# A streaming encoder layer on one core: weights through six 4 KB buffers in place of three of 8 KB

## What is computed

```python
proj = rmsnorm(x, g_mix) @ w_in           # columns q | k | v | g (4 heads x 128) | B | C | h (512 each)
o = rms_scale(retention(rotary(q), rotary(k), v)) * silu(g)     # chunks of 64 frames, a state per head
c = B * short_conv(C * h)                                       # 3 taps
x = x + concat([o, c]) @ w_out
# retrieval, for each frame and each of 8 heads:
q = (rmsnorm(x, g_ffn) @ wq)                     # 1024 x 2048
s1, s2 = q1 @ keys1.T, q2 @ keys2.T              # 128 keys each
eidx, gate = 16 best of the 256 sums of the 16 best of s1 and of s2, softmax
act = gelu(x . u_tab[eidx])                      # 1024 wide rows
x = x + sum(gate * act * v_tab[eidx])
y = rmsnorm(x, g_final)
```

## Time and profile before

| | |
|---|---|
| median of 3 runs | 3038.26 us (3035.58 to 3039.6) |
| the profiled execution | 3035.47 us, of which the span of instructions 3033.6 us |
| granted TensorE clock, mean | 0.846 |
| busy share: PE, PE's weight loads, DVE, ACT, POOL | 76%, 62%, 68%, 67%, 40% |
| moved by DMA | 1226.64 MB, mean 404 GB/s |
| gathers (POOL line 661) | 1056 of 1 MB |
| loads into `stream` | 86 of 1 MB: 26 of w_ret (line 572), 24 of w_conv (line 574), 36 of wq (line 577) |

### The profile page before, as it was taken

One profiled execution on the slowest core, in us unless ns is written; L12 is line 12 of the kernel. 1 busy time (PEld: TensorE's weight loads), 2 busy tenths in 40 slices (PEclk: granted clock), 3 DMA queues, 4 the chain that ended last, 5 costly groups with the idle time before them and its releaser, 6 DMA issues.

```text
span 3033.6 us, 36636 instructions
## 1 busy us (share of the span) xinstructions
PE 2303.3 (76%) x12800; PEld 1880.0 (62%) x12800; DVE 2067.1 (68%) x5112; ACT 2044.8 (67%) x3704; POOL 1228.0 (40%) x1060
## 2 busy tenths in 40 slices
PE   9976887787668887877777877888777766667666
PEld 7765776665557766656566665665556555555555
DVE  2466887566688775666888744566588899955454
ACT  1277666668677566776677666667767777676666
POOL 0133333334333333444443344433344445456653
PEclk9987989998889889987887998989888886666666
DMA  7599999999999999999999999999999999999998
GB/s 301 190 416 397 413 408 414 419 420 413 420 421 409 420 417 415 420 404 420 420 416 406 404 422 419 419 419 396 405 420 420 418 418 409 415 418 419 422 420 333
DMA packets 180568, 1226.64 MB, mean 404 GB/s; under 512 B 20736, under 2 KB 21952, under 8 KB 40736
## 3 DMA queue, kind: packets, MB, share of 16 engines
q0 software_dynamic: 152064, 1107.36, 88.6%
q1 hardware_dynamic: 28032, 116.88, 9.6%
q10 hardware_dynamic: 288, 0.07, 0.0%
HBM read 1219.37 MB, written 4.86 MB: 404 GB/s over the span
## 4 chain that ended last, share of the span: by engine, by line
DMA 35%; DVE 24%; PE 22%; ACT 13%; issue 5%; POOL 1%; DVEq 0%; POOLq 0%; ACTq 0%
DMA ring<-in_uv,idx 35%; DVE ring L1459 12%; PE expert_sum L1116 8%; ACT ring L873 5%; PE mm L914 4%; PE x_ps L976 3%; ACT weights L869 2%; PE mm L1038 2%; PE mm L923 2%; ACT L860 1%; DVE pairs_left L1306 1%; ACT dots L860 1%; DVE pairs_left L1394 1%; DVE top_i L1315 1%; DVE pick_f L1400 1%
## 5 line engine op out<-in xcount | busy, mean ns | idle before, releaser
L661 POOL DMA_INDIRECT ring<-in_uv,idx x1056 | 1227.7, 1163 | 1781.8 <-PE expert_sum L1116 1574.7
L1116 PE MATMUL expert_sum<-ident_sb,ring 128*128 128x128 f32 x8448 | 1367.1, 317 | 581.3 <-ACT ring L873 579.8
L1459 DVE CUSTOM_DVE_ANT_0 ring<-ring,xn 128x1024 f32<-128x1024 f32 x1056 | 1286.7, 1223 | 737.8 <-DMA ring<-in_uv,idx 730.2
L1116 PEld LDWEIGHTS expert_sum<-ident_sb,ring 128*128 128x128 f32 x8448 | 1150.5, 165 | 838.6 <-ACT ring L873 767.9
L873 ACT ACTIVATE ring<-ring,weights 128x1024 f32<-128x1024 f32 x1056 | 1213.2, 1149 | 34.3
L860 ACT ACTIVATE dots<-dots 128x1 f32<-128x1 f32 x1056 | 211.5, 200 | 771.6 <-DVE dots L1459 768.2
L869 ACT ACTIVATE weights<-dots,gate 128x1 f32<-128x1 f32 x1056 | 311.1, 295 | 38.2
L914 PE MATMUL mm<-stream,xn_in 128*128 128x256 f32 (+1 forms) x912 | 258.4, 421 | 71.9 <-ACT qkvg L708 56.3
L1038 PE MATMUL mm<-turn,stream 128*128 128x256 f32 (+2 forms) x1024 | 278.4, 401 | 2.8 <-DVE xn_in L1155 2.8
L914 PEld LDWEIGHTS mm<-stream,xn_in 128*128 128x128 f32 (+1 forms) x912 | 166.9, 199 | 113.7 <-ACT qkvg L708 66.0
L923 PE MATMUL mm<-xn_in,stream 128*128 128x256 f32 (+1 forms) x640 | 183.7, 426 | 34.8 <-ACT conv_tmp L699 22.6
(11 more groups left out here) (233 smaller groups left out, 1517.4 us busy)
## 6 DMA issues: line engine op xcount, KB each, us to landing
stream<-in_wq SPq DMA_DIRECT2D x36, 1024.0 KB, 12.0
stream<-in_w_ret SPq DMA_DIRECT2D x26, 1024.0 KB, 9.4
stream<-in_w_conv SPq DMA_DIRECT2D x24, 1024.0 KB, 11.9
ring<-in_uv,idx POOLq DMA_INDIRECT x1056, 12.3
ring<-in_w_ret SPq DMA_DIRECT2D x7, 1024.0 KB, 12.4
x<-in_x SPq DMA_DIRECT2D x8, 512.0 KB, 8.7
w_out_sb<-in_w_out SPq DMA_DIRECT2D x1, 4096.0 KB, 28.9
out_y<-xn SPq DMA_DIRECT2D x8, 512.0 KB, 11.9
```

What stands on the lines that cost most here:

```text
L661: pool.indirect_dma_start(ring[:, g % RING, :], None, uv, bass.IndirectOffsetOnAxis(ap=rows, axis=0)).then_inc(landed[g % RING], 16)
L1116: ins = pe.matmul(expert_sum[:, c * P:(c + 1) * P], ring[:, g % RING, D + c * P:D + (c + 1) * P], ident_sb[:, :], is_transpose=True, start ...
L1459: dve.tensor_tensor_reduce(u, u, xn[:, t % 3, :], 1.0, 0.0, ALU.mult, ALU.add, dots[:, g % RING:g % RING + 1]).then_inc(dotted, 1)
```

## The change

BUFFERS goes from 3 to 6 and a buffer from 8 KB to 4 KB of a partition. Every item is split: a retention unit into its chunks 0 to 3 and 4 to 7, a convolution pair into its two units, a pass into its halves s = 0 and s = 1. STREAM has 172 items in the order of first use; a second half of a pass is sorted by the slot in which that half begins, both halves of a retention unit by the unit's slot. A half is loaded when the item six before it has been used. The convolution units and the halves of a pass are released one by one, by their own count; the two halves of a retention unit by the same count, at the end of the unit's last use. PE waits for each half where its first chunk stands, also in group 0's units that come through `ring` (there on the same semaphore twice). In the source tensors a half is 4 KB of a partition in one piece.

```diff
--- before.py
+++ after.py
@@ -29,7 +29,7 @@
 QUADS = P // DEC
 TOTAL = TILES * STEPS + STEPS // QUADS
 RING = 7
-BUFFERS = 3
+BUFFERS = 6
 UNIT = 256
 RET_UNITS = 4 * RET // UNIT
 CONV_UNITS = 3 * CH
@@ -251,11 +251,13 @@
 
 
 
+
 STREAM = sorted(
-    [(USES[j][use_at(j, "ret", u, GROUPS[j][0])][3], 0, "ret", j, u) for j in range(1, 4) for u in range(RET_UNITS)]
-    + [(USES[j][use_at(j, "ChB"[2 * i % 3], 2 * i)][3], 0, "conv", j, i) for j in range(4) for i in range(CONV_UNITS // 2)]
-    + [(USES[0][use_at(0, "ret", RING, t)][3], 0, "ret", 0, t) for t in GROUPS[0]]
-    + [(p[3], 1, "wq", n, p[1]) for n, p in enumerate(PASSES)])
+    [(USES[j][use_at(j, "ret", u, GROUPS[j][0])][3], 0, "ret", j, u, s)
+     for j in range(1, 4) for u in range(RET_UNITS) for s in range(2)]
+    + [(USES[j][use_at(j, "ChB"[v % 3], v)][3], 0, "conv", j, v, 0) for j in range(4) for v in range(CONV_UNITS)]
+    + [(USES[0][use_at(0, "ret", RING, t)][3], 0, "ret", 0, t, s) for t in GROUPS[0] for s in range(2)]
+    + [(p[3] + KC * s // p[4], 1, "wq", n, p[1], s) for n, p in enumerate(PASSES) for s in range(2)])
 ITEM = {x[2:]: i for i, x in enumerate(STREAM)}
 
 
@@ -295,7 +297,7 @@
         ring = sb("ring", [P, RING, 2 * D])
         w_out_sb = sb("w_out_sb", [P, KC, D])
         keys_sb = sb("keys_sb", [P, BLK, NK])
-        stream = sb("stream", [P, BUFFERS, 2 * D])
+        stream = sb("stream", [P, BUFFERS, D])
         xn_in = sb("xn_in", [P, KC * wide])
         qkvg = sb("qkvg", [P, 2, 4 * RET])
         conv_out = sb("conv_out", [P, CH, wide])
@@ -550,17 +552,17 @@
 
             def used(i):
 
-                kind, j, n = STREAM[i][2:]
+                kind, j, n, s = STREAM[i][2:]
                 if kind == "wq":
-                    return pass_end(j) - 1, queried, 2 * (j + 1)
+                    return PASSES[j][3] + (KC * (s + 1) - 1) // PASSES[j][4], queried, 2 * j + s + 1
                 if kind == "ret" and j == 0:
                     q = use_at(0, "ret", RING, n)
                     return USES[0][q][3] + 2, projected, q + 1
-                q = use_at(j, "ret", n, GROUPS[j][-1]) if kind == "ret" else use_at(j, "ChB"[(2 * n + 1) % 3], 2 * n + 1)
+                q = use_at(j, "ret", n, GROUPS[j][-1]) if kind == "ret" else use_at(j, "ChB"[n % 3], n)
                 return USES[j][q][3] + 2, projected, USES_BEFORE[j] + q + 1
 
             def load_stream():
-                for i, (_, _, kind, j, n) in enumerate(STREAM):
+                for i, (_, _, kind, j, n, s) in enumerate(STREAM):
                     if i < BUFFERS:
                         yield FIRST
                     else:
@@ -569,13 +571,12 @@
                         sp.wait_ge(semaphore, count)
                     dst = stream[:, i % BUFFERS, :]
                     if kind == "ret":
-                        sp.dma_start(dst, w_ret[n if j else RING]).then_inc(stream_in[i % BUFFERS], 16)
+                        source = w_ret[n if j else RING][:, s * D:(s + 1) * D]
                     elif kind == "conv":
-                        sp.dma_start(dst.rearrange("p (u n) -> p u n", u=2),
-                                     w_conv[2 * n:2 * n + 2].rearrange("u p n -> p u n")).then_inc(stream_in[i % BUFFERS], 16)
+                        source = w_conv[n]
                     else:
-                        sp.dma_start(dst.rearrange("p (b k n) -> p b k n", b=2, k=KC),
-                                     wq[2 * n:2 * n + 2].rearrange("b p k n -> p b k n")).then_inc(stream_in[i % BUFFERS], 16)
+                        source = wq[2 * n + s].rearrange("p k n -> p (k n)")
+                    sp.dma_start(dst, source).then_inc(stream_in[i % BUFFERS], 16)
 
             def load_consts():
                 yield FIRST + 1
@@ -878,13 +879,13 @@
 
         @block.tensor
         def _(pe):
-            def item_in(kind, j, n, t=None):
+            def item_in(kind, j, n, s=0, t=None):
                 if kind == "ret" and j == 0 and n < RING:
                     pe.wait_ge(ret_in[n], 16)
-                    return ring[:, n, :]
+                    return ring[:, n, s * D:(s + 1) * D]
                 if kind == "ret" and j == 0:
                     n = t
-                i = ITEM[kind, j, n]
+                i = ITEM[kind, j, n, s]
                 pe.wait_ge(stream_in[i % BUFFERS], 16 * (i // BUFFERS + 1))
                 return stream[:, i % BUFFERS, :]
 
@@ -905,22 +906,23 @@
                     bank = bank_of(j, q)
                     if kind == "ret":
                         if t == GROUPS[j][0] or j == 0:
-                            weight = item_in("ret", j, unit, t).rearrange("p (k n) -> p k n", k=KC)
+                            weight = [None, None]
                         n, at = rows_of(t), column(t)
                         for k in range(KC):
                             yield slot if slot in range(4) else slot + k // 3
                             if k in (0, KC // 2):
+                                if weight[k // 4] is None:
+                                    weight[k // 4] = item_in("ret", j, unit, k // 4, t).rearrange("p (k n) -> p k n", k=4)
                                 pe.wait_ge(xnT_copied, 2 * x_turn(t) + 1 + k // (KC // 2))
-                            ins = pe.matmul(bank[0:n, 0:UNIT], xnj[:, k, at:at + n], weight[:, k, :],
+                            ins = pe.matmul(bank[0:n, 0:UNIT], xnj[:, k, at:at + n], weight[k // 4][:, k % 4, :],
                                             start=(k == 0), stop=(k == KC - 1))
                     else:
                         if unit == 0:
                             pe.wait_ge(xnT_copied, 2 * x_turn(ORDERS[j][-1]) + 2)
-                        if unit % 2 == 0:
-                            item = item_in("conv", j, unit // 2).rearrange("p (u k n) -> p u k n", u=2, k=KC)
+                        item = item_in("conv", j, unit).rearrange("p (k n) -> p k n", k=KC)
                         for k in range(KC):
                             yield slot + k // 3
-                            ins = pe.matmul(bank[:, 0:w], item[:, unit % 2, k, :], xnj[:, k, :],
+                            ins = pe.matmul(bank[:, 0:w], item[:, k, :], xnj[:, k, :],
                                             start=(k == 0), stop=(k == KC - 1))
                     ins.then_inc(projected, 1)
 
@@ -1031,11 +1033,12 @@
                         by_act, by_dve = taken_all(j)
                         pe.wait_ge(act_took, by_act)
                         pe.wait_ge(dve_took, by_dve)
-                    weight = item_in("wq", m, h).rearrange("p (b k n) -> p b k n", b=2, k=KC)
                     for s in range(2):
+                        yield slot + KC * s // pace
+                        weight = item_in("wq", m, h, s).rearrange("p (k n) -> p k n", k=KC)
                         for k in range(KC):
                             yield slot + (KC * s + k) // pace
-                            ins = pe.matmul(query_bank(m, s), weight[:, s, k, :], xnT_of_pass(m)[:, k, :],
+                            ins = pe.matmul(query_bank(m, s), weight[:, k, :], xnT_of_pass(m)[:, k, :],
                                             start=(k == 0), stop=(k == KC - 1))
                         ins.then_inc(queried, 1)
 
```

## The result

| | before | after |
|---|---|---|
| median | 3036.85 us (22 runs) | 3041.76 us (22 runs) |
| ratio | | 1.0017, 95% interval 1.0011 to 1.0023 |
| the profiled execution, its span | 3035.47, 3033.6 us | 3042.09, 3040.0 us |

The median rose by 4.9 us, inside the 0.2% that I had called no change, with an interval (+3.3 to +7.0 us) that excludes none at all. The forecast had +2.1.

What follows compares the result with a forecast made beforehand. The DMA engines were taken as the bound after about 120 us. Pieces +2.9, completions +0.7, PE's waits 0 and the stall -1.5 sum to +2.1 on a median of 3038.3: 3040.4 us, range 3034.5 to 3046.5.

Steps and rivals of the forecast that it cites:

- The number: Whole kernel: median of three runs 3038.3 us plus 2.1, so 3040.4 us expected; 0.2%, 6 us, counts as no change.
- The bound: Middle of the kernel: the 16 DMA engines are full, share 1.01 at 414 to 416 GB/s; before about 120 us PE bounds.
- PE's added waits: First 120 us, where PE is the bound: 24 added waits cost 0, at most +0.7 us.
- the first gather: Sign at the end of PE's first part: still starts at 119.3 us; over 1 us later would mean the waits cost.
- Smaller pieces, +2.9: The 26 w_ret loads go from 8 KB to 4 KB packets, 1.8 engine-us more each: +2.9 us (2.7 to 3.2).
- Completions, +0.7: 86 added DMAs bring 1376 completion packets on the engines: +0.7 us, between 0 and 1.5.
- The stall, -1.5: PE's 6.94 us idle before group 1's retention unit 5 costs 1.9 us; shorter waits give back 1.5 (0 to 1.9).
- The rival of late halves spreading the stall: Slots 102 to 121: four late halves each cost 1.9 us or more, 3047.6 us in all; chance 0.16.
- The fixed part of every DMA: All 86 added DMAs: each pays a fixed 2.4 us, 206 us together, 3244 us in all; chance 0.01.
- Gathers gain: Gathers beside the 26 w_ret loads land 1.8 us earlier; a sixth on the path gives 3032.4 us; chance 0.06.

Runs made afterwards that it cites:

- the direct comparison: Kernel before with every item loaded by two 0.5 MB DMAs (1.0014, +4.3 us) against kernel before with only w_ret in 4 KB pieces (1.0011, +3.3 us).
- The repeat: The changed kernel run once more, nothing altered, against the kernel before: 1.0015 (1.0006 to 1.0024).
- small pieces alone: Kernel before with only the 26 w_ret loads in two 4 KB pieces a partition, still one 1 MB DMA each: 1.0011 (1.0002 to 1.0020), +3.3 us.

## Why the prediction was right, point by point

- **The number**: the median came within 1.4 us of the forecast 3040.4, in part by luck. The forecast stood on a median of three runs that lay 1.4 us above that of all 22, and the rise itself was 4.9 us where +2.1 was foretold. The missing 2.8 are the stall's 1.5, which did not come back, and small loads that cost 4 to 5 us and not 3.6.
- **The bound**: right. The DMA share stays at 1.01, PE's added waits are not seen, the first gather didn't move later, and the packets' time accounts for the change's.
- **Smaller pieces, +2.9**: right in size. The time rose by 2.8 to 3.3 us and the packets of SP's queue took 2.9 more. That the time agrees so closely is partly luck, since this run holds a stall longer by 2.3 us. Taken on 60 other loads the same price was 6.8 us. Nine of these come before 118 us, where the engines are not the bound, which leaves 5.7; SP's queue gave back 4.6, the gathers took 2.2 of that, and the time fell by 0.5. For 1 KB pieces the price held to within a third. So the step "a queue's share in a window is time on the path" left out what the gathers' packets do. Why the gathers' packets lengthen is open.
- **Completions, +0.7**: as packets they are what was foretold, 9.5 ns each for SP's queue at the mean, 0.8 us for 1376. As the whole price of 86 DMAs the term is too small. The runs show 0.02 to 0.07 us a DMA, 2 to 6 us for 86, and the direct comparison gives 2.0, above the bound of 1.5 that I gave.
- **The stall, -1.5**: the step that failed is "I take 1.5 of the 1.9 us back". Its mechanism was right to within 0.7 us of the foretold moments, and step 104 came 8.8 us earlier, but step 128 came only 0.1 us earlier, less than the lead of 0.9 that step 96 had. The repeat shows no gain either, and with 4.9 us of the stall put back the kernel was level, in an interval of some 3 us. A gain under that is not excluded. The rival of late halves spreading the stall didn't come: waits of 1.32 and 2.57 us, covered as worked out.
- **The fixed part of every DMA** (the rival with the rule of the Trainium skill's page "DMA: Bandwidth & Descriptors", section "Bandwidth"): 2.4 us a DMA would have been 206; the trace and the runs disagree with that size by a factor of 30 or more, but agree in the direction, and that direction is one of the two places where my sum was short.
- **Gathers gain**: the end of the kernel shows none. With small pieces alone step 96 comes 6.2 us earlier than before, but it comes 3.9 earlier too in the run that leaves the w_ret loads alone and cuts 42 others, and by step 128 it is 2.5 us later; so nothing can be read from it.

## What to carry to other kernels

Before splitting a buffer for earlier release, work out from the order of use how far each load is ahead; here 83 of 86 were never near, and the split could give at most the 1.9 us of one stall, while a further DMA was paid on all 86 and smaller pieces on 26. With two thirds of the buffer space the same split was worth 23 to 25 us. And to test what more DMAs cost, keep the partitions that each of them covers.

## What was not expected of the hardware

DMAs of 16 partitions by 4 KB, sixteen in the place of one, made the gathers beside them slower too: 337 GB/s with full engines where 416 is usual, 0.435 us lost for each. Pieces of 8 KB in place of 4 KB took 4% less of the engines in the queue's row for one load, and no gain in the time could be measured. And a load's time to land beside gathers follows its pieces: a megabyte of w_ret took 9.4 us at the median in pieces of 8 KB, 12.0 in 4 KB and 25.9 in 1 KB.
